# Expert tables by partition: one contiguous range of experts per partition, wider DMA runs for expert_v and the gates

## The reference, cut to what matters

```
qry = (xf @ w_query).reshape(T, 8, 2, 128)
sa, sb = qry[:, :, 0] @ sub_keys_a.T, qry[:, :, 1] @ sub_keys_b.T          # 128 scores each
va, ia = top_k(sa, 16); vb, ib = top_k(sb, 16)
top_s, pos = top_k(va[..., :, None] + vb[..., None, :], 16)                # of 256 pairs
experts = (ia * 128 + ib) at pos                                           # 16384 experts
gates = softmax(top_s)
act = gelu(einsum('tkd,td->tk', expert_u[experts], x))
out = einsum('tk,tkd->td', gates * act, expert_v[experts])
```

## Time and profile before

| | us |
|---|---|
| time, median of 3 runs | 4118.97 (4109.92 to 4119.53) |
| span of the profiled execution | 4056.0 |
| span of `apply` in it | 1922 to 4056 |
| TensorE busy | 3497.1 |
| VectorE busy | 2775.1 |
| ScalarE busy | 907.0 |
| GpSimd busy | 1556.6 |

### The profile page before, as it was taken

The page is one execution under the profiler, slowest core; times in us unless marked ns, Lnnn a source line. Parts: engine busy times, 40 slices in busy tenths (PEclk is TensorE's granted clock), DMA queues, the critical chain, the costliest instruction groups (busy, mean ns, idle before and its releaser), DMA issues.

```text
span 4056.0 us, 39947 instructions
## 1 busy us (share of the span) xinstructions
PE 3497.1 (86%) x13253; PEld 1966.8 (48%) x13253; DVE 2775.1 (68%) x5292; ACT 907.0 (22%) x1917; POOL 1556.6 (38%) x1400
## 2 busy tenths in 40 slices
PE   7999958888765688985899889899999898989995
PEld 3444435555552588885444444444444444444442
DVE  1222234566442378887698888988888988987787
ACT  0111115566321025546100111101110111101110
POOL 0000000000165000000565666666666666667675
PEclk9999966998877799998899999999999899999997
DMA  8222032110264456563998999999999999999997
GB/s 302 88 90 89 34 118 74 48 44 32 49 190 142 169 204 255 209 249 132 348 360 307 395 376 388 360 373 391 386 386 335 393 386 384 358 376 403 397 400 278
DMA packets 345757, 1044.35 MB, mean 257 GB/s; under 512 B 32160, under 2 KB 82640, under 8 KB 341392
## 3 DMA queue, kind: packets, MB, share of 16 engines
q0 software_dynamic: 184336, 667.00, 43.9%
q1 hardware_dynamic: 161216, 374.80, 25.4%
HBM read 974.27 MB, written 67.14 MB: 257 GB/s over the span
## 4 chain that ended last, share of the span: by engine, by line
DVE 20%; DMA 14%; POOL 8%; DVEq 5%; issue 4%; PE 1%; SPq 0%; ACT 0%; POOLq 0%
DMA pick_v<-in_expert_v,ids 13%; DVE acc L2486 10%; DVE e_junk L2470 6%; POOL pick_u L2296 4%; DVEq L2481 4%; POOL pick_v L2304 4%; PE psH L2356 1%; DVE e_away L1771 1%; DVE e_found L1774 1%; DVE e_W L2435 1%; DMA e_u<-in_expert_u 1%; DVEq L1737 0%; DVE e_spare L1732 0%; DVE e_ia L1731 0%; DVE e_va L1734 0%
## 5 line engine op out<-in xcount | busy, mean ns | idle before, releaser
L2356 PE MATMUL psH<-XT,e_uT 128*128 128x512 f32 x2048 | 966.0, 613 | 122.3 <-ACT e_uT L2393 122.3
L2369 PE MATMUL psY<-e_v,e_W 128*128 128x512 f32 x2048 | 891.0, 597 | 19.3 <-DVE e_W L2435 19.3
L2486 DVE SCALAR_TENSOR_TENSOR acc<-pick_v,pick_w,acc 128x1024 f32<-128x1024 f32 x571 | 733.5, 1285 | 231.8 <-DMA pick_v<-in_expert_v,ids 189.6
L2296 POOL DMA_INDIRECT pick_u<-in_expert_u,ids x576 | 712.1, 1236 | 393.6 <-DVE pick_dot L2470 259.0
L2304 POOL DMA_INDIRECT pick_v<-in_expert_v,ids x576 | 658.7, 1144 | 281.5 <-issue 161.3
L2470 DVE CUSTOM_DVE_ANT_0 e_junk<-pick_u,x_rows 128x1024 bf16<-128x1024 f32 x576 | 702.9, 1220 | 26.2 <-DMA pick_u<-in_expert_u,ids 14.0
L2369 PEld LDWEIGHTS psY<-e_v,e_W 128*128 128x128 f32 x2048 | 392.1, 192 | 515.6 <-issue 487.9
L2356 PEld LDWEIGHTS psH<-XT,e_uT 128*128 128x128 f32 x2048 | 380.2, 197 | 510.6 <-issue 369.7
L385 PE MATMUL ps_p<-w_in_sb,hT 128*128 128x512 f32 x1008 | 441.0, 597 | 0.0
L385 PEld LDWEIGHTS ps_p<-w_in_sb,hT 128*128 128x128 f32 x1008 | 190.9, 191 | 231.8 <-issue 231.7
L2393 ACT ACTIVATE e_uT<-psU 128x512 f32<-128x512 f32 x256 | 149.0, 594 | 638.0 <-PE psU L2348 637.9
(11 more groups left out here) (453 smaller groups left out, 3888.1 us busy)
## 6 DMA issues: line engine op xcount, KB each, us to landing
w_query_sb<-in_w_query SPq DMA_DIRECT2D x36, 2048.0 KB, 8.1
e_u<-in_expert_u SPq DMA_DIRECT2D x128, 512.0 KB, 7.2
e_v<-in_expert_v SPq DMA_DIRECT2D x128, 512.0 KB, 11.1
G_d<-G_stage SPq DMA_DIRECT2D x16, 2048.0 KB, 12.0
e_g<-G_d SPq DMA_DIRECT2D x16, 2048.0 KB, 26.1
w_ada<-in_w_ada POOLq DMA_DIRECT2D x16, 1024.0 KB, 10.1
w_in_sb<-in_w_in SPq DMA_DIRECT2D x7, 2048.0 KB, 19.3
pick_u<-in_expert_u,ids POOLq DMA_INDIRECT x576, 8.6
```

Source lines behind the costliest of these rows:

```text
L2296: pool.indirect_dma_start(gu[:, i % NGU, :], None, io["expert_u"][0], bass.IndirectOffsetOnAxis(ids[:, q % 2, j:j + 1], 0)).then_inc(pu_in ...
L2356: m = pe.matmul(psH[a % 2][:, :], uT[:, a % 2, j, :], XT[:, j, :], start=j == 0, stop=j == KD - 1)
L2369: m = pe.matmul(psY[i % NY][:, :], W[:, (b * NBK + t) % NW, k * P:(k + 1) * P], v[:, t, half_cols(half)], start=t == 0, stop=t == NBK - 1)
L2486: dve.scalar_tensor_tensor(out=sums_q, in0=gv[:, i % NGV, :], scalar=wgt[:, m % 2, o:o + 1], in1=sums_q, op0=ALU.mult, op1=ALU.add).then_i ...
```

## The change

Partition p now holds the experts 128p to 128p + 127, and tile a is made of the experts 128p + a. Rows of one tile of `expert_u` are 512 KB apart in HBM. Tiles a and a + 1 of `expert_v` are neighbours for each partition, so they are loaded together, 8 KB per partition. To bring G into the same order, the operands of `spread` change places; and G_d is laid out [partition, block, group of tokens, tile in the block, token], so that a gate load is one run of 16 KB per partition and a store is 16 runs of 1 KB per partition, 16 KB apart.

```
+NBK = 8
-        G_d = dram("G_d", (TD // HT, P, NK, HT))
+        G_d = dram("G_d", (P, NK // NBK, TD // HT, NBK, HT))
@@ keep
-                sp.dma_start(G_d[q], gs[:, q % NS_, :, :]).then_inc(g_stored[q % NS_], 16)
+                sp.dma_start(G_d[:, :, q, :, :].rearrange("p m n t -> p m (n t)"), gs[:, q % NS_, :, :].rearrange("p (m n) t -> p m (n t)", n=NBK)).then_inc(g_stored[q % NS_], 16)
@@ spread
-                    m = pe.matmul(psG[:, i % 2, t, :], ob[:, i % NO, t, :], oa[:, i % NO, t, :], start=True, stop=True)
+                    m = pe.matmul(psG[:, i % 2, t, :], oa[:, i % NO, t, :], ob[:, i % NO, t, :], start=True, stop=True)
@@ apply
-    NBK, NU, NW, NY = 8, 3, 9, 4
+    NU, NW, NY, VT = 3, 9, 4, 2
-        v_in = [sem(f"e_v_in{i}") for i in range(NBK)]
+        v_in = [sem(f"e_v_in{i}") for i in range(NBK // VT)]
-        u_rows = io["expert_u"][0].rearrange("(a b) d -> a b d", b=P)
-        v_rows = io["expert_v"][0].rearrange("(a b) d -> a b d", b=P)
+        u_rows = io["expert_u"][0].rearrange("(b a) d -> a b d", b=P)
+        v_rows = io["expert_v"][0].rearrange("(b a) d -> b a d", b=P)
@@ load_v
-            def load_v(b, t):
-                if b >= 1 and t == 0:
+            def load_v(b, n):
+                if b >= 1 and n == 0:
                     sp.wait_ge(y_out, UNITS * b)
-                sp.dma_start(v[:, t, :], v_rows[b * NBK + t]).then_inc(v_in[t], 16)
+                sp.dma_start(v[:, n * VT:(n + 1) * VT, :], v_rows[:, b * NBK + n * VT:b * NBK + (n + 1) * VT, :]).then_inc(v_in[n], 16)
@@ load_gates
-                sp.dma_start(g[:, :, :, :], G_d[:, :, b * NBK:(b + 1) * NBK, :].rearrange("q b a t -> b q a t")).then_inc(g_in, 16)
+                sp.dma_start(g[:, :, :, :], G_d[:, b]).then_inc(g_in, 16)
@@ the loop of SP
-                    load_v(b, 2 * (t - 4))
-                    load_v(b, 2 * (t - 4) + 1)
+                    load_v(b, t - 4)
@@ sums
-                        pe.wait_ge(v_in[t], 16 * (b + 1))
+                        if t % VT == 0:
+                            pe.wait_ge(v_in[t // VT], 16 * (b + 1))
```

More of the change, by code:

```diff
@@ L2203, in apply @@
         set_up = sem("e_setup")
-        u_in, g_in, v_in = [sem(f"e_u_in{i}") for i in range(NU)], sem("e_g_in"), [sem(f"e_v_in{i}") for i in range(NBK)]
+        u_in, g_in, v_in = [sem(f"e_u_in{i}") for i in range(NU)], sem("e_g_in"), [sem(f"e_v_in{i}") for i in range(NBK // VT)]
         u_turned, u_kept, h_out, h_act, weighed, y_out, y_added = (sem(f"e_{n}") for n in ("u_turned", "u_kept", "h_out", "h_act", "weighed", "y_out", "y_added"))
```

## The result

| | before | changed |
|---|---|---|
| time, median of 12 runs | 4113.52 us (4108.58 to 4119.53) | 4124.74 us (4119.09 to 4130.63, and one of 6197.66) |
| ratio of the changed kernel to the kernel before | | 1.0027, 95% interval 1.0017 to 1.0036 |
| the same, measured again (`after_here`, below) | | 1.0016, interval 1.0005 to 1.0028 |
| profiled execution | 4056.0 us span | 4122.5 us span, 4124.29 us measured |

The account below looks back on a forecast made before the run. DMA was taken to bound the products at 410 GB/s, VectorE and TensorE together the sums. Terms -4.0 + 0 + 1.3 - 6.0 + 6.0 = -2.7 us gave 4116 us, with an 8-in-10 range of 4078 to 4157.

Parts of the forecast that it names:

- part 5: Fifteen later gate loads, at the start of the sums: 16 KB packets delay gathers; +6 us (0 to +26).
- rival B: Starved gathers: gate packets delay expert_v gathers in the sums, TensorE then waits in the products; +38, 4157 us, chance 0.17.
- The lag: Gathers held back by a later gate load in the sums: at worst 2.8 gathers, 4.6 us.
- The turns: Two DMA queues with work alternate on the engines, turn by turn; 8 gate turns per engine instead of 128.
- part 4: First gate load, start of `apply`: fewer gate turns bring TensorE's second tile earlier; -6.0 us (0 to -8.3).
- Its sign: VectorE waiting for expert_v gathers in the first 10 us of the sums, with a total above 189.6 us.
- Part 1: expert_v loaded by pairs in 8 KB runs: higher DMA rate in the products; -4.0 us (-4.7 to 0).
- Part 2: expert_u rows 512 KB apart, expert_v pairs at the same pitch: no slower reading; 0 us (0 to +84).
- Rival C: Pitch: rows 512 KB apart read more slowly, taking DMA time from gathers in the products; +81, 4200 us, chance 0.09.
- Part 3: Gate stores in routing, 1 KB packets: only the last store, ending the phase, costs; +1.3 us (at most +8.5).
- Rival A: Relief: every freed DMA microsecond moves the end, leaving VectorE ahead for the products; -28, 4091 us, chance 0.32.

Follow-up runs that it names:

- after_here: The changed kernel with no edit, measured again in a later set of runs: 4123.51 us, ratio 1.0016 to the kernel before.
- gates_only: Kernel before with the new order of G_d alone (gate loads in 16 KB runs, stores in 1 KB runs): 4064.41 us, ratio 1.0029.
- pitch_pairs: Changed kernel with the old G_d, expert_v still loaded by pairs in 8 KB runs: 4047.53 us, ratio 0.9981 to the kernel before.
- before_again: The kernel before with no edit, run and profiled a second time: 4051.66 us, ratio 0.9996.
- before_v5: Kernel before with five buffers for expert_v gathers in place of four, each issued one pick earlier: 4065.55 us, ratio 0.9874.
- pitch_only: Changed kernel with the old G_d and expert_v loaded tile by tile, leaving only the 512 KB row distance: 4050.55 us, ratio 0.9988 to the kernel before.
- first_wide: Kernel before with block 0's gates in their own tensor, loaded in 16 KB runs, the other fifteen loads at 1 KB: 4048.43 us, ratio 0.9987.

## Why the prediction was wrong

**The step that failed is part 5**, the fifteen later gate loads: +6 us as predicted, some 16 us as measured. gates_only is +11.8 us; it has the lead of the first load, 5.6 us, and pays 1.6 us more in `routing` (587.0 for 585.4), so the later loads cost 11.8 + 5.6 - 1.6 = 15.8 us, 1.1 us a block. (By the two profiles alone `apply` is 15.5 us longer, which would make it 21.) The mechanism was in the text, and as rival B at 0.17; the term was sized wrong. With 15.8 for 6.0 the sum comes to +7 us, and the ratios measured are +7 us (1.0016) and +11 us (1.0027). gates_only and pitch_pairs together give 1.0010; the 1.0016 agrees with that, and the rest of the 1.0027 stays open. The lag was worked out at 2.8 gathers, measured 2.3. But I set it against all of VectorE's 2.9 us of slack and then took a quarter of the rest. The one sums stretch read, 2428 to 2483 us, has no wait for gathers; that only said that they came just in time there, not that they had time to spare, and it was not typical: over fifteen blocks VectorE waits 43.4 us for gathers in the sums already before the change (before_again). The lead of the expert_v gathers was short, as before_v5 shows, and I passed over it in half a sentence. The turns, one for one, were right; only the 204 ns of part 4 spread the landing time of 26.1 us over 128 turns as if the packets began at the issue. Rival B itself (4157 us) overstated the price: 47 us where 15.8 were lost. Its sign was there, but weak: VectorE's waits for expert_v gathers are 194.6 us for the 189.6 of the earlier trace rows.

**Part 1**, pairs: -4.0 us predicted. pitch_pairs less pitch_only is -3.0 us, not resolved by the intervals. The rate rose as assumed: 2550 to 2570 us of the changed kernel moved 8.28 MB, for the 8.21 of the earlier trace rows.

```profile
DMA packets 1848, 8.28 MB, mean 414 GB/s; under 512 B 206, under 2 KB 206, under 8 KB 1468
```

**Part 2**, rows 512 KB apart: 0 predicted; pitch_only is 0.9988, at most a small gain and no loss. The mean 4 KB packet of q1 in `apply` took 166 ns in pitch_only and 165 ns in before_again. Rival C is out, and so, for this pitch and these reads into SBUF, is the 3% that comes out of what the Trainium skill gives for copies between HBM tensors ("DMA: Bandwidth & Descriptors", "Latency and other measured facts"): 11 us would be a ratio of 1.0027, outside the interval 0.9977 to 1.0000.

**Part 3**, the last store: +1.3 predicted. SP's wait for it went from 6.0 to 7.2 us, and its 2 MB from the 62.1% of the earlier trace rows to 77.3% of 8 us, 6.2 us by the sum I had made:

```profile
SPq L1914 <- DMA G_d<-G_stage: 7.2, 1, 7.2
```
```profile
q1 hardware_dynamic: 2064, 2.10, 77.3%
```

The other fifteen stores cost nothing visible.

**Part 4**, the first load: -6.0 predicted, -6.3 measured between the first two tiles (9.7 for 16.0 us), -5.6 at block 0 of gates_only, and first_wide, 4 us faster than before, shows that most of it lasts to the end.

**Rival A** had it that freed DMA time moves the end. It didn't: by gates_only's figures the gates took less DMA time and the kernel was slower.

## What to carry to other kernels

A transfer that no one waits for can still be too fast. Where gathers are just in time, look at how long the other queue's packets are, not only at what they need in all: here the load that was cheapest for the DMA engines was the dearest for the kernel, and 1 KB packets, spread over 26 us, were right for it. "No wait in the profile" is not slack: find the lead of a transfer (issue to use, less issue to landing) before a burst is put in front of it; and where the lead is short, one more buffer can be worth more than the layout in question (52 us against 11 us here).

## What the runs showed of the hardware

- Two queues that both have work share the DMA engines about one packet for one at the three lengths tried: 115 records of the gathers to 103 of 16 KB gate packets in 5 us, 398 to 446 at 4 KB in 8 us, 174 to 187 at 1 KB in 2 us. So the queue with long packets gets most of the bytes. In 8 us after a gate load the gathers (4 KB packets) moved 2.32, 1.83 and 1.09 MB beside gate packets of 1, 4 and 16 KB, and the load landed after 26.1, 14.6 and 11.1 us in the median.
- Tiles of 128 rows of 4 KB that lie 512 KB apart were read as fast as tiles in one piece.
- The same program ran at two levels in different sets of runs (medians of 4052 to 4053 us, and of 4113.52 and 4118.67). The first profile and that of the changed kernel differ by 61.2 us before `routing` begins; what makes the difference in the sample phases is open.
